# First projection block on one Trainium2 core: four norms ahead of the copies, the first weights rounded in quarters, low-part products of two tiles behind both tiles' other products

## The reference

```python
u = rms_norm(h, norm_mix_g[l])
z = u @ w_in[l]
xa = z[..., :D_LRU]
...
xa = causal_depthwise_conv(xa, conv_w[l], conv_b[l])
ha = rg_lru(xa, w_rg[l], b_rg[l], w_ig[l], b_ig[l], lru_lambda[l]) * jax.nn.gelu(ya)
```

## Time and profile before

| what | value |
|---|---|
| device time, median of 3 runs | 889.17 us (888.45 to 889.28) |
| profiled execution, its own time | 888.04 us |
| its span, first to last instruction | 886.3 us |
| PE busy | 836.9 us (94%) |
| DVE busy | 342.7 us (39%) |
| ACT busy | 272.0 us (31%) |
| POOL busy | 81.3 us (9%) |

### The profile page before, as it was taken

The page is one execution under the profiler, slowest core; times in us unless marked ns, Lnnn a source line. Parts: engine busy times, 40 slices in busy tenths (PEclk is TensorE's granted clock), DMA queues, the critical chain, the costliest instruction groups (busy, mean ns, idle before and its releaser), DMA issues.

```text
span 886.3 us, 10339 instructions
## 1 busy us (share of the span) xinstructions
PE 836.9 (94%) x4281; PEld 530.6 (60%) x4281; DVE 342.7 (39%) x478; ACT 272.0 (31%) x397; POOL 81.3 (9%) x61
## 2 busy tenths in 40 slices
PE   4999999999999999999999999889898898999996
PEld 4888888788888888536535353353352353533675
DVE  6899449962652626411020120101100102013964
ACT  7666347633332235202010100101001001003767
POOL 3436370000000000000000000000000000000000
PEclk9999999999999999999999999999999999999998
DMA  9222222211425755999999999999999999998802
GB/s 260 96 93 95 95 95 95 95 48 54 183 95 225 297 237 199 357 416 424 402 429 427 427 427 427 428 428 427 428 427 426 429 426 428 428 422 322 343 1 95
DMA packets 45334, 253.85 MB, mean 286 GB/s; under 512 B 8868, under 2 KB 9960, under 8 KB 31976
## 3 DMA queue, kind: packets, MB, share of 16 engines
q1 hardware_dynamic: 42696, 248.21, 69.1%
q0 software_dynamic: 2304, 4.20, 1.2%
q10 hardware_dynamic: 288, 0.79, 0.3%
HBM read 246.89 MB, written 10.49 MB: 290 GB/s over the span
## 4 chain that ended last, share of the span: by engine, by line
PE 75%; DMA 17%; DVE 2%; issue 2%; ACT 2%; SPq 1%; DVEq 0%; POOLq 0%; ACTq 0%
PE bank L1419 74%; DMA ring<-in_w_down_e_dram 14%; DMA r<-in_w_ple_gate_dram 2%; PE bank L1632 1%; DMA r<-in_x_dram 1%; SPq L621 1%; DMA expert_rows<-r,row_i 0%; DVE r_rounded L418 0%; PE bank L1484 0%; ACT ring_rounded L943 0%; ACT L1016 0%; ACT junk L734 0%; DVE ring_rounded L1051 0%; ACT r_rounded L743 0%; DVE pick L1220 0%
## 5 line engine op out<-in xcount | busy, mean ns | idle before, releaser
L1419 PE MATMUL bank<-ring_rounded,ring_rounded 128*128 128x512 f32 (+1 forms) x696 | 245.0, 389 | 1.9 <-DVE r_rounded L1051 1.9
L1419 PE MATMUL bank<-r_rounded,ring_rounded 128*128 128x512 f32 (+1 forms) x744 | 234.4, 389 | 1.0 <-DVE ring_rounded L1051 0.9
L1419 PEld LDWEIGHTS bank<-r_rounded,ring_rounded 128*128 128x128 f32 x744 | 138.8, 188 | 30.8 <-DVE ring_rounded L1051 1.2
L1419 PEld LDWEIGHTS bank<-ring_rounded,ring_rounded 128*128 128x128 f32 x696 | 130.5, 188 | 29.6 <-DVE r_rounded L1051 2.3
L1419 PE MATMUL bank<-ring,gain 128*64 128x512 f32 x472 | 119.7, 612 | 11.6 <-issue 11.6
L1419 PE MATMUL bank<-ring,junk 128*64 128x512 f32 x472 | 115.5, 592 | 0.0
L1419 PE MATMUL bank<-ring,hT 128*64 128x512 f32 x400 | 109.3, 607 | 5.0 <-DMA ring<-in_w_down_e_dram 5.0
L1419 PEld LDWEIGHTS bank<-ring,gain 128*64 128x64 f32 x472 | 36.6, 140 | 79.8 <-issue 76.9
L1419 PEld LDWEIGHTS bank<-ring,junk 128*64 128x64 f32 x472 | 37.6, 137 | 71.4 <-issue 71.3
L1419 PEld LDWEIGHTS bank<-pick,r_rounded 128*128 128x128 f32 x576 | 72.6, 199 | 9.9 <-issue 8.5
L1419 PE MATMUL bank<-pick,r_rounded 128*128 128x256 f32 x576 | 74.7, 292 | 3.9 <-DVE pick L1220 3.9
(11 more groups left out here) (216 smaller groups left out, 761.7 us busy)
## 6 DMA issues: line engine op xcount, KB each, us to landing
ring<-in_w_up_e_dram SPq DMA_DIRECT2D x29, 2048.0 KB, 29.1
ring<-in_w_gate_e_dram SPq DMA_DIRECT2D x24, 2048.0 KB, 27.7
ring<-in_w_down_e_dram SPq DMA_DIRECT2D x22, 2048.0 KB, 31.4
ring<-in_w_in_dram SPq DMA_DIRECT2D x18, 1024.0 KB, 7.3
r<-in_w_gate_e_dram SPq DMA_DIRECT2D x5, 2048.0 KB, 27.5
r<-in_w_down_e_dram SPq DMA_DIRECT2D x4, 2048.0 KB, 33.9
ring<-in_w_down_e_dram SPq DMA_DIRECT2D x7, 1024.0 KB, 23.2
ring<-in_w_up_e_dram SPq DMA_DIRECT2D x6, 1024.0 KB, 10.8
```

The costliest lines, as they stand in the source:

```text
L1419: return nc.tensor.matmul(*a, **k)
```

## The change

ACT takes the squares and roots of all four row tiles first, then copies six transposed banks, rounds the first quarter of the weights, copies the last two banks and rounds the other three quarters. The two 128x2048 roundings of the first block have become four of 128x1024; POOL and DVE are told of a half only when its second quarter is written. The transposes use six banks and DVE takes the low parts of `uT` in an order that frees the two reused banks first. PE starts its products when the high parts of `uT` are there and takes the first tile's high-weight products, then the second tile's, then the low-weight products of both. `keep_busy` before the first product goes from 11 to 7 transposes.

```diff
+        FIRST_BANKS = (4, 5, 6, 7, 1, 2, 4, 6)
+        FIRST_LOWS = (0, 2, 4, 1, 3, 5, 6, 7)
...
             for i in range(TT):
                 act.wait_ge(x_in[i], 16)
                 norm(i, xin[:, i, :])
-                if i >= 2:
-                    copy_transposed(2 * i - 4, uT_high, (4, 5, 6, 7))
-                    copy_transposed(2 * i - 3, uT_high, (4, 5, 6, 7))
-            split_high(act, 0, 0)
-            for q in range(2 * TT - 4, 2 * TT):
-                copy_transposed(q, uT_high, (4, 5, 6, 7))
-            split_high(act, 0, 1)
+
+            def split_first(step):
+
+                h, part = step // 2, slice(step % 2 * 2, step % 2 * 2 + 2)
+                if step % 2 == 0:
+                    act.wait_ge(half_in[0][h], 16)
+                ins = nc.scalar.activation(high_half(0, h)[:, part, :], whole_half(0, h)[:, part, :], ACT.Copy)
+                ins.then_inc(first_high, 1)
+                if step % 2 == 1:
+
+                    act.wait_ge(first_high, step + 1)
+                    act.sem_inc(high_ready, 1)
+
+            for q in range(2 * TT - 2):
+                copy_transposed(q, uT_high, FIRST_BANKS)
+            split_first(0)
+            for q in range(2 * TT - 2, 2 * TT):
+                copy_transposed(q, uT_high, FIRST_BANKS)
+            for step in range(1, 4):
+                split_first(step)
...
             for i in range(TT):
                 normalise(i, i, xin[:, i, :], xin[:, i, :])
-                if i >= 2:
-                    uT_split(2 * i - 4)
-                    uT_split(2 * i - 3)
-            for q in range(2 * TT - 4, 2 * TT):
-                uT_split(q)
+            for q in FIRST_LOWS:
+                uT_split(q, banks=FIRST_BANKS)
...
-            keep_busy(11)
-            pe.wait_ge(ut_low, 2 * TT)
+            keep_busy(7)
+            pe.wait_ge(ut_ready, 2 * TT)
+
+            def first_tiles():
+
+                def product(t, k, low, still, **flags):
+                    w = (low_half if low else high_half)(0, k // 4)[:, k % 4, t * P:(t + 1) * P]
+                    return mm(bank[t][:, :], w, still[:, k, :], **flags)
+
+                for t in range(2):
+                    if t == 1:
+
+                        pe.wait_ge(ut_low, 2 * TT)
+                    for g in range(2):
+                        for still in (uT_high, uT_low):
+                            if t == 0 and still is uT_low:
+                                pe.wait_ge(ut_low, 2 * TT)
+                            for k in range(4 * g, 4 * g + 4):
+                                if t == 0 and still is uT_high:
+                                    pe.wait_ge(first_high, k // 2 + 1)
+                                product(t, k, False, still, start=(k == 0 and still is uT_high), stop=False)
+                for t in range(2):
+                    for k in range(KD):
+                        if t == 0 and k % 4 == 0:
+                            pe.wait_ge(*lows_at(0, k // 4))
+                        ins = product(t, k, True, uT_high, start=False, stop=(k == KD - 1))
+                    ins.then_inc(tile_done, 1)
```

More of the change, by code:

```diff
@@ L287, in build @@
         ut_low = sem("ut_low")
+        first_high = sem("first_high")
         tile_done = sem("tile_done")
@@ L742, in copy_transposed @@
                 dst_k = dst[:, 4 * h:4 * h + 4, (i % TT) * P:(i % TT + 1) * P]
-                nc.scalar.activation(dst_k, bank[banks[q % 4]][:, :].rearrange("p (k t) -> p k t", k=4),
+                nc.scalar.activation(dst_k, bank[banks[q % len(banks)]][:, :].rearrange("p (k t) -> p k t", k=4),
                                      ACT.Copy).then_inc(ut_ready, 1)
@@ L1044, in normalise, with uT_split @@
                                        op1=ALU.mult).then_inc(norm_done, 1)
-            def uT_split(q, high=uT_high, low=uT_low):
+            def uT_split(q, high=uT_high, low=uT_low, banks=(4, 5, 6, 7)):
                 i, h = q // 2 % TT, q % 2
@@ L1050, in uT_split @@
                 part = slice(4 * h, 4 * h + 4), slice(i * P, (i + 1) * P)
-                v.tensor_tensor(low[:, part[0], part[1]], bank[4 + q % 4][:, :].rearrange("p (k t) -> p k t", k=4),
+                v.tensor_tensor(low[:, part[0], part[1]], bank[banks[q % len(banks)]][:, :].rearrange("p (k t) -> p k t", k=4),
                                 high[:, part[0], part[1]], ALU.subtract).then_inc(ut_low, 1)
@@ L1427, in transpose_rows @@
                     pe.wait_ge(norm_done, i + 1)
-                if q % (2 * TT) >= 4:
-                    pe.wait_ge(ut_low, q - 3)
+                if banks[q] in banks[0:q]:
+                    pe.wait_ge(ut_low, FIRST_LOWS.index(banks.index(banks[q])) + 1)
                 for k in range(4):
-                    ins = nc.tensor.transpose(bank[banks[q % 4]][:, k * P:(k + 1) * P],
+                    ins = nc.tensor.transpose(bank[banks[q]][:, k * P:(k + 1) * P],
                                               src[:, i % TT, (4 * h + k) * P:(4 * h + k + 1) * P], ident[:, :])
@@ L1438, in keep_busy @@
                 for _ in range(products):
-                    nc.tensor.transpose(bank[2][:, 0:P], ident[:, :], ident[:, :])
+                    nc.tensor.transpose(bank[0][:, 0:P], ident[:, :], ident[:, :])
             for q in range(2 * TT):
@@ L1443, in _ @@
                     keep_busy(7)
-                transpose_rows(q, xin, (4, 5, 6, 7))
+                transpose_rows(q, xin, FIRST_BANKS)
             pe.wait_ge(small_in, 16 * 6)
             nc.tensor.transpose(bank[3][:, 0:NV], vecs[0:NV, :], ident[0:NV, 0:NV]).then_inc(vec_psum, 1)
-            keep_busy(11)
-            pe.wait_ge(ut_low, 2 * TT)
+            keep_busy(7)
[21 more added lines that the diff above has]
+                    ins.then_inc(tile_done, 1)
             def lru_gates(c):
@@ L1510, in places @@
                 ins.then_inc(places_psum, 1)
+            first_tiles()
             for t, (kind, c) in enumerate(tiles):
+                if t < 2:
+                    continue
                 n = block_of[kind, c]
```

## The result

The changed kernel takes 891.57 us, the median of 20 runs (889.18 to 896.76). The kernel before, run beside it, takes 889.15, also a median of 20 (887.86 to 891.20). The ratio is 1.0038, with an interval of 1.0028 to 1.0047: 0.38% slower.

The account below looks back on a forecast made before the run. The prediction took PE to bound the dense stage, with DVE's chain exactly as late at 56.2 us. POOL's half starting before `diag_low` adds 6.0 to the median of 889.17, giving 895.2 us, range 890.3 to 896.8.

Parts of the forecast that it names:

- What bounds the kernel: PE alone counts in the dense stage; at 56.2 us, before tile 3's gate products, DVE is exactly as late.
- PE's start: PE's first product starts at 17.7 us instead of 19.31, 1.6 earlier.
- POOL's half and the negation: POOL's first weight half runs 18.1 to 22.65, 1.65 later, holding DVE's 128x8 negation until 22.7 instead of 21.03.
- A tie near 28.1: DVE's `diag_low` moves from 26.45 to 28.1 us, as good as together with POOL's second weight half at 28.05.
- Two to one: Odds that POOL's second weight half starts ahead of DVE's `diag_low` near 28.1 us.
- DVE first: `diag_low` starts ahead of POOL's half near 28.1 us: +1.65 us, 890.8; chance 0.27.
- POOL first: POOL's half starts ahead of `diag_low`, tile 3's gate products wait until 62.2: +6.0 us, 895.2; chance 0.60.
- rival 3: PE's clock falls to 0.50 behind its wait from 58.9 to 62.2: +6.0 + 1.4, 896.6; chance 0.06.
- the first stall: PE idle for 4.3 us before its first gate products, which start at 38.4 instead of 35.80.
- the second stall: PE waits from 58.9 to 62.2 us, up to 3.3, before tile 3's gate products.
- rival 4: The negation slips in ahead of POOL, PE's 1.6 lead dies at 56.20: 889.2 less 0.26 at most; chance 0.03.
- rival 5: A PE lead of 1.8 carries through, needing DVE's tile 3 low part at 53.6, not 55.45: 887.3; chance 0.04.

Follow-up runs that it names:

- the first profile: The changed kernel unedited, the one execution profiled among its 20 runs: 889.18 us.
- experiment 7: Changed kernel; DVE takes both first-block low halves, POOL's second-block halves in four released pieces, ACT rounds half (1, 1) behind its convolution 1 part: 887.12 us.
- experiment 9: The changed kernel unedited, profiled four more times: 895.79, 894.03, 893.95 and 894.89 us.
- experiment 1: The changed kernel with one wait added, so that POOL takes its half (1, 0) only behind DVE's `diag_low`: 890.39 us, ratio 1.0025.
- Experiment 2: The changed kernel with one wait added, so that DVE takes `diag_low` only behind POOL's half (1, 0): 895.37 us, ratio 1.0072.
- experiment 3: The kernel before with only one wait added: DVE takes `diag_low` behind POOL's half (1, 0): 894.12 us, ratio 1.0069.
- experiment 4: The changed kernel with PE's first product waiting for both rounded first weight halves and all activation low parts: 893.25 us, ratio 1.0055.
- experiment 5: The changed kernel with DVE, not POOL, also taking the low part of weight half (0, 0): 889.27 us, ratio 1.0007.
- experiment 6: Changed kernel; DVE takes both first-block low halves, POOL's second-block halves come in four pieces released under DVE's convolutions and reciprocal: 889.66 us, ratio 1.0003.
- experiment 8: The kernel before with POOL's second-block halves in four released pieces and ACT's rounding of half (1, 1) moved behind convolution 1: 888.78 us, ratio 0.9997.

## Why the prediction came out as it did

- **What bounds the kernel: right.** "At 56.2 us DVE is exactly as late as PE." Every kernel here whose DVE chain is late at that point passes the lateness on, whatever PE did before, and only experiment 7, with the chain early, keeps a lead of PE's (0.92 us there).
- **PE's start: right.** Forecast 17.7, measured 17.72 (1.37 / 11 is 0.12 and not the 0.11 that I used; the starts of the seven transposes are 0.10 apart). Rounding 128x1024 took 1.05 (forecast 1.06). At quarter 4, where I had no wait, the weight loads stood for 0.33 us; PE waits for DVE later anyway, so it cost nothing here; in experiment 7, where PE's lead counts, such waits took 0.58 and 0.44.
- **POOL's half and the negation: right.** Forecast 18.1 to 22.65 and a negation until 22.7; measured 18.19 to 22.81 and 22.85. The Trainium skill, SBUF — State Buffer, section "Who interferes with whom", says that the second to issue blocks until the first ends. The rows agree in both directions: the negation ends 0.04 behind POOL, and of the two long instructions the second ends 0.08 to 0.13 sooner than the end of the first and its own time give (DVE's lasted 6.41 to 6.62 with POOL first, POOL's 6.68 with DVE first).
- **A tie near 28.1: right.** Measured 28.29 against 28.31.
- **"Two to one" for POOL: the step that failed.** I argued that all errors of `diag_low`'s time lay on the late side. It was late, by 0.19 in the first profile. But the weights' landing, on which POOL's start hangs, was later as well, by 0.27 (ACT's rounding at 26.32 against 26.05 of the earlier trace rows). Over all fourteen profiles, of before, after and the experiments, that rounding starts between 26.01 and 26.61: the one profile that I had was nearly the earliest, and I only wrote that it "can move either way". The race is drawn anew in each run. By its times DVE won eleven of the twenty; the four runs of experiment 9, on one chip, POOL won all. Times near 893.3 can't be told apart for certain, since the forced DVE first of experiment 1 has 893.12 and 893.5 too. Thirteen of twenty-four for POOL does not contradict odds of two to one. What failed is the use of them: I put the whole median on one outcome, and the median of such a mixture lies with whichever side has more runs. It came to 891.57, between my 890.8 and my 895.2, and 3.6 below the forecast; my range held because it covered both orders. That the two orders make the groups is shown for the upper one by four profiles, POOL first at 893.95 to 895.79, and rests for the lower one on a single profile, DVE first at 889.18, and on experiment 1, whose forced order gives its median again, 890.39. Experiment 2, which forces the other order, gives 895.37, 1.5 above the upper group's median.
- **The size of DVE first: right.** Forecast +1.65; +1.75 at tile 3, +1.24 at the end in the group's median, +1.8 in experiment 1.
- **The size of POOL first: right at tile 3, less sure at the end.** Forecast +6.0 and gate products at 62.2; measured 62.21 to 62.58. At the end the forced order is at +6.8 (experiment 2) and +5.6 (experiment 3), the upper group at +4.7. "I let a shift of PE's stream reach the end one for one" holds to about a microsecond only, since a single execution moves by that much: the first profile is 1.75 late at tile 3 and 1.1 at the end (span 887.4 against 886.3). A part of such differences is the clock in the routing stage: its fall over the second batch costs 1.5 to 2.4 us in some executions and is absent in others of the same kernel, as experiment 9 shows. In the first profile it is absent. I had no term for it. How often it came in the unprofiled runs is not known, so what gives the group less than the forced order stays open.
- **The clock's fall (rival 3): it happens, and where I put it.** I wrote that PE gives back a fall behind the first stall, and that only one behind the second stays. Experiments 2 and 9 show the first, with the wait at tile 3 shortened for it (1.99 and 0.58 to 1.92, where I had 3.3), experiment 4 the second. The 6 in 100 were for a fall behind the second stall, and none of the four POOL-first profiles of the changed kernel had one; behind the first stall it came in each POOL-first profile with an early PE. It did not set the time there. The Trainium skill, TensorE: Matmul & The Clock Gate, in its summary table, speaks of gaps of more than about 3 us; the first stall (3.65 to 4.01 us) agrees, but experiments 4 and 5 show falls behind 2.85 and 1.87, so a gap below its figure was not safe here.
- **The change does not reach PE (rival 4): fell, with a twist.** The negation can slip in ahead of POOL, as it did in experiment 2 and in three of the four profiles of experiment 9, and it does not help, since the next instruction of the same kind is held.
- **Faster (rival 5): fell for this kernel.** I asked for DVE's low part of tile 3 at 53.6 and named POOL's halves and ACT as what stood against it. Experiment 7 gets near it (53.79) by moving just these two, and measures 887.12 where I had 887.3 "if it did". That the times agree so well is luck in part: I had let a lead of 1.8 carry through, and PE is 0.92 ahead at tile 3.

## What to carry to other kernels

Before valuing an engine's earlier start, find the next place where it waits for another engine with almost no slack; here 0.26 us of waiting at 56.20 said that 1.6 us won at the start would be lost (the changed kernel and experiment 5 lost them). When a long SBUF-to-SBUF instruction of POOL moves, follow what DVE has in its queue under it, however short, and look for instructions that now fall together: here a race within some 0.3 us made the times fall in two groups, and a forecast should then be a mixture, with the spread of both sides taken from several profiles. Cut such POOL work to fit under DVE instructions that have an operand in PSUM, and check at once which engine is the next to be late.

## What the runs showed of the hardware that I had not expected

- A race of 0.02 to 0.34 us between DVE and POOL was worth 3.4 us of 890 between the groups' medians (893.83 against 890.39). In the two profiles that differ in its outcome and else agree, the first and the first of experiment 9, DVE stood at 28.29 and 28.27 and the weights' rounding at 26.32 and 26.11: the landing of the load decided it.
- The kernel before, in whose profile `diag_low` is 1.6 us ahead of POOL, still spread over 4.4 us in 18 runs (887.04 to 891.48) and 5.5 in 35; experiment 7 spread over 1.7 in 12. The routing stage's fall of the clock, 1.5 to 2.4 us where it meets the second batch, is of a size to give part of such a spread; that it does is not shown.
- POOL's 128x1024 pieces took 2.40 to 2.42 us and DVE's three convolution instructions 2.31 to 2.32 in experiments 6 to 8, where they run side by side; alone in the kernel before, DVE's took 2.31 at 38.65. These DVE instructions, which have one operand in PSUM, and POOL did not hold each other; that it is the operand in PSUM was not tested by itself.
- The low clock came behind short idle times. These are PE's rows ahead of 3.4 us at or near 0.50, in experiment 4 and in experiment 5:

```profile
62.27 0.50 PE L1433 MATMUL bank<-ring_rounded,ring_rounded 128*128 128x512 f32 x1 [2.85 <-DVE ring_rounded L1118]
```

```profile
56.76 0.50 PE L1434 MATMUL bank<-ring_rounded,ring_rounded 128*128 128x512 f32 x1 [1.87 <-DVE ring_rounded L1119]
```

  Waits of 1.45 to 1.67 at the same place (experiments 1, 2, 3 and 6, the first profile of after and three of experiment 9) brought none. That is no safe figure either: in the kernel before the clock fell at 351.6, and the longest idle time of PE in the 6 us ahead of it was 0.65, among transposes and matmuls of 128x36. An early PE that only waits longer is thus not free: the wait itself can cost another 1.7 us (experiment 5). Experiment 7 has no such wait, but neither has experiment 8, which spread over 3.8 us, so this does not explain why experiment 7 spread least.
